# Products of constants in TensorE's waits: norms, feed-forward entries, two recurrence levels and the heads' loop

## The chip, the cores and the metric

The kernel runs on one core of one Trainium2 chip. Its time is the device time of one execution in microseconds (us); of the kernel before, three runs took 2835.75, 2836.42 and 2836.65, median 2836.42. A core has five engines that run their own instruction streams in order and wait for each other by semaphores: TensorE (PE; its weight loads stand as PEld), VectorE (DVE), ScalarE (ACT), GpSimd (POOL) and SyncE (SP), which issues transfers.

## What is computed

Two networks of two layers each, one behind the other, on 256 tokens of width 1024, in f32.

```python
def first_block(x, mem, ...):
    for l in range(2):
        x = x + 0.5 * swiglu(rms_norm(x, ffn1_norm[l]), ffn1_w_gu[l], ffn1_w_down[l])   # 1024 -> 2816 -> 1024
        h = rms_norm(x, mix_norm[l]); z = h @ w_in[l]
        y_a = dilated_attention(...) @ w_att_branch[l]
        o_b = hgrn2_recurrence(...)            # a gated recurrence over the tokens, 8 heads
        x = x + (sigmoid(gate_a) * y_a + sigmoid(gate_b) * y_b) @ w_mix_out[l]
        x = x + cross_attention(rms_norm(x, xattn_norm[l]), rms_norm(mem, mem_norm[l]), ...)
        x = x + 0.5 * swiglu(rms_norm(x, ffn2_norm[l]), ...)
    return rms_norm(x, final_norm)

def second_block(x, c, ...):
    for l in range(2):
        h = rmsnorm(x, norm_g[l, 0]) * (1 + sc1) + sh1
        x = x + 0.5 * g1 * swiglu_2(h, ...)
        h = rmsnorm(x, norm_g[l, 1]) * (1 + sc2) + sh2
        qa, ka, va, qb, kb, vb, qi, ki, wi, qc, kc, vc = split(h @ w_in[l])
        o = concat(moba_attention(qa, ka, va), dsa_attention(qb, kb, vb, qi, ki, wi),
                   stick_breaking_attention(qc, kc, vc))      # 4, 4 and 8 heads of 64
        x = x + g2 * (rms(o) * out_g[l] @ w_out[l])
        h = rmsnorm(x, norm_g[l, 2]) * (1 + sc3) + sh3
        x = x + 0.5 * g3 * swiglu_2(h, ...)
```

## The kernel before

All weights come from HBM as one stream of 1 MB tiles through a ring of four slots. A weight product has f32 accuracy out of three matmuls of a faster format: ScalarE copies a tile to its high part (`w_hi`, L320), VectorE subtracts for the low part (`ring_lo`, L327), and `triple` (L329) multiplies high by high, high by low and low by high. Nearly all of TensorE's work is such triples. Products of two activations, and sums by a constant matrix, are plain f32 matmuls; the trace shows each of these as two matmuls.

Each engine's program is written out by hand in one function per block and engine (`one_pe`, `two_pe`, `two_act` and so on); the order in it is the order on the engine, and `wait_ge` lines set what waits for what.

A norm works on four quarters of `x` (token half b, column half): ScalarE squares them with a running sum (`square`), VectorE forms the variance, both the reciprocal root; VectorE scales a quarter (L598 where there is a shift), TensorE transposes it (`flip_x`, L524: wait for `h_scaled`, four transposes, count `xt_done`), ScalarE copies the transposed quarter to `h_hi` (`h_high`, L391), VectorE subtracts for `h_lo` (L576). The engines do these in an order of their own for each norm. For the norm behind block two's first feed-forward ScalarE's is `shift_z_act` (L509):

```python
            h_high(act, n, 0, 4)
            square(act, n, 2)
            square(act, n, 3)
            rstd_act(act, n, 1)
```

A feed-forward (`ffn_pe`) begins with `first_three` (L832): for the first token half b=0 eight triples over two weight tiles and four over a third, then the transposes of the second half (`flip_x(pe, n, 1, base)`, last where `turn_last` is set, as in block two), then the same triples for b=1. Its four calls in block two are the first and second feed-forward of either layer, called entries below; block one's second feed-forward is the one with `FFN_B`.

`level` (L1268) is one of eight levels of block one's recurrence: TensorE runs two tiles of projections, waits for VectorE's and ScalarE's exponentials (`e_ready`) and multiplies them for eight heads.

The heads' loop of `two_pe` takes eight pairs of heads, one ordinary and one stick-breaking. Per turn TensorE transposes the probabilities of one head into bank 6 (`flip`, L2317), multiplies scores of a later pair, sums the logarithms of the stick-breaking head into bank 1 (`sums`, L2325) and weighs the values. Bank 6 is free again when ScalarE has copied it (L2516, counted by `pt_ready`); the exponentials (L2499) are counted by `exp_ready`. Bank 1 is free when VectorE has taken its argument from it (L2721, `arg_ready`). After every second pair, TensorE transposes the normed outputs back (`turn_back`, L2364).

Of the kernel before, what the change touches and what calls it, by code (L numbers as in the profile page):

```python
# [30 lines left out]
T = 256  # L31
D = 1024
KD = D // P
DEPTH = 2
# [30 lines left out]
FFN_B = X_O + 4  # L65
# [12 lines left out]
FFN_C = 0  # L78
# [7 lines left out]
FFN_D = Z_O + 4  # L86
# [95 lines left out]
def program(nc, x_in, mem_t, pos, c_row, gain_rows, stream, ada, vec, con, lmask, out):  # L182
    with ExitStack() as ctx:
# [105 lines left out]
        S = type("S", (), s)  # L289
# [9 lines left out]
        def nth(which, count):  # L299

            return base.get(which.num, 0) + count
# [27 lines left out]
        def triple(out, w, x, start, stop, group=False):  # L329

            for n, (a, b) in enumerate(((w[0], x[0]), (w[0], x[1]), (w[1], x[0]))):
                mm = nc.tensor.matmul(out, a, b, start=start and n == 0, stop=stop and n == 2,  # L332
                                      skip_group_check=group)
            return mm

        def weights(p, a, b):
# [494 lines left out]

        def first_three(pe, p, n, base, banks, done, turn_last):  # L832

            for b in range(2):
                for k in range(KD):
                    if b == 0 and k % 4 == 0:
                        pe.wait_ge(S.w_lo_ready, p + k // 4 + 1)
                    if k % 4 == 0:
                        pe.wait_ge(S.h_ready, nth(S.h_ready, 4 * n + 2 * b + k // 4 + 1))
# [9 lines left out]
                mm = half_pair(pe, p + 2, 0, (banks[0] + 2, banks[1] + 2), h2, b)  # L849
                if b == 0 and turn_last:  # L850
                    flip_x(pe, n, 1, base)
            mm.then_inc(S.tile_done, 1)
# [32 lines left out]

        def ffn_pe(pe, p0, f, n, shift, between=None, near=None, after=None):

# [25 lines left out]

            first_three(pe, p0, n, 4, (0, 1), S.gu_done, shift)
            if between:
# [335 lines left out]
        def one_pe(pe, l):  # L1251
# [16 lines left out]
            def level(i):  # L1268

                if i < LEVELS:  # L1270
                    pe.wait_ge(S.e_ready, nth(S.e_ready, i + 1))
# [195 lines left out]
            out_pairs(pe, X_O, 4, (o_hi, o_lo), S.att_ready, HEADS, lambda: flip_x(pe, 3, 0, 4))  # L1467
            ffn_pe(pe, FFN_B, 1, 3, False, near=(lambda: flip_x(pe, 4, 0, 4)) if l < DEPTH - 1 else None)

# [718 lines left out]
        pt2 = prob_t  # L2188
        OUT_BANK = (7, 3, 7, 4)
        o_tok = hk[:].rearrange("p k t -> p (k t)").rearrange("p (j n) -> p j n", j=4)  # L2190
        stat = e_buf[1][:].rearrange("p k t -> p (k t)")
# [18 lines left out]
        def two_pe(pe, l):  # L2210
            FFN_C, Z_QI, Z_V, Z_O, FFN_D = tiles_2(l)
            if l == 0:
                flip_x(pe, 0, 0, 4)
            ffn_pe(pe, FFN_C, 0, 0, True, after=lambda: flip_x(pe, 1, 0, 4))

            flip_x(pe, 1, 1, 4)

            def tile(n):
# [98 lines left out]
            def flip(n):  # L2317
                pe.wait_ge(S.exp_ready, nth(S.exp_ready, n + 1))
                if n >= 1:
                    pe.wait_ge(S.pt_ready, nth(S.pt_ready, n))  # L2320
                for c, at in enumerate((0, P, 2 * P)):
                    mm = nc.tensor.transpose(ps[:, 6, c * P:(c + 1) * P], prob_2[n % 3][:, at:at + P], ident)
                mm.then_inc(S.pt_done, 1)

            def sums(c):  # L2325

                pe.wait_ge(S.l_ready, nth(S.l_ready, c + 1))
                if c >= 1:
                    pe.wait_ge(S.arg_ready, nth(S.arg_ready, c))
                ll = st[:, 4 + c % 2, :]  # L2330
                nc.tensor.matmul(ps[:, 1, 0:T], C(C_TRI, P), ll[:, 0:T], start=True, stop=False,
# [95 lines left out]
            flip_x(pe, 2, 0, 4)  # L2427
            ffn_pe(pe, FFN_D, 1, 2, True, after=(lambda: flip_x(pe, 3, 0, 4)) if l < DEPTH - 1 else None)

# [675 lines left out]
```

## Time and profile before

| | |
|---|---|
| profiled execution | 2836.47 us |
| its span, first to last instruction | 2834.4 us |
| PE | 2767.2 us busy, 98% |
| DVE | 1951.5 us, 69% |
| ACT | 1364.6 us, 48% |
| mean granted TensorE clock | 0.991 |

Of the chain of waits that ended last, 83% is TensorE and 9% VectorE. A busy share says that an engine has work at hand, not that it works at full clock: the granted clock stands apart, as a share of 2.4 GHz. In the timeline, a bracket at the end of a row is the time that the engine was idle before it, with what ended the wait. The ends of matmuls are modelled and overlap the next one's start, so of many like matmuls the distance of the starts is the price of one.

### The profile page before, as it was taken

The page shows a single profiled execution, that of the slowest core. Times are in us where ns is not written, and L with a number is a line of the kernel's source. Part 1 is how long each engine was busy: PE and PEld are TensorE (multiplying, and loading weights), DVE is VectorE, ACT ScalarE, POOL GpSimd, SP SyncE. Part 2 cuts the span into 40 slices and gives each one's busy share as a digit, 9 for nine tenths or more (in the row PEclk, how much of TensorE's full clock was granted, in tenths as well). Part 3 has the DMA queues.
Part 4 walks back from the last instruction along what each step waited for, and adds up shares of the span by engine and source line. Part 5 has one row for each costly group of instructions (what it writes and reads, how often), then busy time and mean ns, then how long its engine had stood idle before and what let it go on. Part 6 is the DMA issues. An engine that isn't in the chain of part 4 may idle for free.

```text
span 2834.4 us, 37832 instructions
## 1 busy us (share of the span) xinstructions
PE 2767.2 (98%) x16120; PEld 2426.3 (86%) x16120; DVE 1951.5 (69%) x2187; ACT 1364.6 (48%) x1562; POOL 228.7 (8%) x201
## 2 busy tenths in 40 slices
PE   8999999999999999999999999999999999999999
PEld 6889999998888889999998887888878878788787
DVE  6768876655666678876655667667876676777644
ACT  5444545455445444545455444444644444446433
POOL 0000420000000000420000000003000000030000
PEclk9999999999999999999999999999999999999999
DMA  8655433445776654433446676663266676442554
GB/s 304 258 220 183 153 120 134 171 164 200 267 265 236 257 214 179 149 134 134 162 159 230 254 257 247 253 224 135 103 238 251 246 264 258 183 149 77 197 187 148
DMA packets 82038, 564.42 MB, mean 199 GB/s; under 512 B 9072, under 2 KB 10576, under 8 KB 15952
## 3 DMA queue, kind: packets, MB, share of 16 engines
q1 hardware_dynamic: 66272, 465.47, 44.9%
q0 software_dynamic: 15600, 96.55, 9.1%
q8 instruction: 127, 2.08, 0.3%
q14 instruction: 39, 0.32, 0.0%
HBM read 560.86 MB, written 1.12 MB: 198 GB/s over the span
## 4 chain that ended last, share of the span: by engine, by line
PE 83%; DVE 9%; ACT 3%; POOL 2%; DMA 2%; issue 1%; SPq 0%; POOLq 0%; ACTq 0%; DVEq 0%
PE ps L332 75%; DVE ring_lo L327 3%; ACT w_hi L320 2%; PE ps L899 1%; DMA rows<-mod_rows 1%; POOL qk L2038 1%; PE ps L1287 1%; POOL rope_a L2034 1%; PE ps L530 1%; DVE a_hg L1806 1%; PE ps L1416 0%; PE ps L1442 0%; DVE e L993 0%; DVE e L1786 0%; DVE e L1785 0%
## 5 line engine op out<-in xcount | busy, mean ns | idle before, releaser
L327 DVE TENSOR_TENSOR ring_lo<-ring,w_hi 128x2048 fp32r<-128x2048 f32 x422 | 974.0, 2310 | 478.6 <-ACT w_hi L320 464.2
L320 ACT ACTIVATE w_hi<-ring 128x2048 fp32r<-128x2048 f32 x422 | 806.2, 1910 | 308.5 <-PE ps L332 187.7
L332 PE MATMUL ps<-w_hi,h_hi 128*128 128x512 f32 (+1 forms) x1920 | 731.7, 381 | 17.6 <-DVE h_lo L576 9.2
L332 PE MATMUL ps<-w_hi,h_lo 128*128 128x512 f32 (+1 forms) x1920 | 719.2, 375 | 0.0
L332 PE MATMUL ps<-ring_lo,h_hi 128*128 128x512 f32 (+1 forms) x1920 | 718.7, 374 | 0.0
L332 PEld LDWEIGHTS ps<-w_hi,h_hi 128*128 128x128 f32 x1920 | 365.3, 190 | 84.9 <-DVE ring_lo L327 10.3
L332 PE MATMUL ps<-h_hi,w_hi 128*128 128x256 f32 x1488 | 431.0, 290 | 1.3 <-DVE h_lo L576 1.3
L332 PE MATMUL ps<-h_lo,w_hi 128*128 128x256 f32 x1488 | 422.7, 284 | 0.0
L332 PE MATMUL ps<-h_hi,ring_lo 128*128 128x256 f32 x1488 | 422.6, 284 | 0.0
L332 PEld LDWEIGHTS ps<-w_hi,h_lo 128*128 128x128 f32 x1920 | 364.8, 190 | 65.3
L332 PEld LDWEIGHTS ps<-ring_lo,h_hi 128*128 128x128 f32 x1920 | 365.5, 190 | 61.1 <-issue 1.0
L332 PEld LDWEIGHTS ps<-h_hi,w_hi 128*128 128x128 f32 x1488 | 287.2, 193 | 6.3 <-issue 5.9
L332 PEld LDWEIGHTS ps<-h_lo,w_hi 128*128 128x128 f32 x1488 | 287.4, 193 | 2.8 <-issue 2.4
L332 PEld LDWEIGHTS ps<-h_hi,ring_lo 128*128 128x128 f32 x1488 | 287.1, 193 | 0.0
L332 PE MATMUL ps<-w_hi,g_hi 128*128 128x512 f32 x576 | 224.6, 390 | 1.6 <-DVE g_lo L1083 1.6
L332 PE MATMUL ps<-w_hi,g_lo 128*128 128x512 f32 x576 | 224.1, 389 | 0.0
L332 PE MATMUL ps<-ring_lo,g_hi 128*128 128x512 f32 x576 | 224.1, 389 | 0.0
L993 DVE CUSTOM_DVE_ANT_0 e<-e,val 128x1024 f32<-128x1024 f32 x154 | 181.6, 1220 | 5.7 <-ACT val L1000 5.7
L1041 ACT ACTIVATE g_hi<-ps 128x512 fp32r<-128x512 f32 x80 | 47.7, 597 | 227.6 <-PE ps L899 227.6
L981 POOL DMA_DIRECT2D e<-ada x77 | 40.7, 529 | 1121.8 <-DVE mod_sum L993 826.6
L332 PEld LDWEIGHTS ps<-w_hi,g_hi 128*128 128x128 f32 x576 | 108.1, 188 | 24.7 <-DVE g_lo L1083 2.4
L332 PEld LDWEIGHTS ps<-w_hi,g_lo 128*128 128x128 f32 x576 | 108.1, 188 | 22.5
(359 smaller groups left out, 3430.2 us busy)
## 6 DMA issues: line engine op xcount, KB each, us to landing
ring<-stream SPq DMA_DIRECT2D x438, 1024.0 KB, 4.8
e<-ada POOLq DMA_DIRECT2D x77, 1024.0 KB, 5.9
rows<-mod_rows POOLq DMA_DIRECT2D x18, 512.0 KB, 6.5
rows<-gain_rows POOLq DMA_DIRECT2D x8, 512.0 KB, 4.6
val<-c_row POOLq DMA_DIRECT2D x4, 512.0 KB, 5.2
x<-x_in SPq DMA_DIRECT2D x4, 256.0 KB, 6.7
mem<-mem_t SPq DMA_DIRECT2D x1, 1024.0 KB, 16.1
out_t<-x SPq DMA_DIRECT2D x4, 256.0 KB, 2.1
```

The source lines that it names most:

```text
L320: nc.scalar.activation(hi_of(p), ring[:, p % RING, :], ACT.Copy).then_inc(S.w_hi_ready, 1)
L327: nc.vector.tensor_tensor(lo_of(p), ring[:, p % RING, :], hi_of(p).bitcast(F32), ALU.subtract).then_inc(S.w_lo_ready, 1)
L332: mm = nc.tensor.matmul(out, a, b, start=start and n == 0, stop=stop and n == 2, skip_group_check=group)
L530: mm = nc.tensor.transpose(ps[:, base + q, j * P:(j + 1) * P], xs[:, b, at:at + P], ident)
L899: mm = nc.tensor.transpose(ps[:, bank, a * T + b * P:a * T + (b + 1) * P], g_f[:, i % 2, b, a * P:(a + 1) * P], ident)
L981: pool.dma_start(e_buf[(i + 1) % 2][:].rearrange("p k t -> p (k t)"), ada[l * 2 * PER_FFN + first + i]).then_inc(ada_loaded[(i + done) % 2 ...
L993: ins = nc.vector.tensor_tensor_reduce(part, part, silu_c, 1.0, 0.0, ALU.mult, ALU.add, mod_sum[:, at + n:at + n + 1])
L1041: nc.scalar.activation(g_hi[:, g_slot(i - 1), :], ps[:, 2 * ((i - 1) % 2), :], ACT.Copy).then_inc(S.ghi_ready, 1)
L1287: mm = nc.tensor.matmul(ps[:, 4 + 2 * g + j // 2, at:at + n], sta[:, hd, t * P:(t + 1) * P], right, start=True, stop=True)
L1806: ins = nc.vector.copy_predicated(dst.rearrange("p a (g two c) -> p a g two c", two=2, c=c)[:, :, :, 1, :], upper(mask, c).unsqueeze(1).br ...
L2034: nc.gpsimd.tensor_tensor(rope_a[:], part, cos1[:].unsqueeze(1).broadcast_to([P, 2, T]), ALU.mult).then_inc(S.pool_chain, 1)
L2038: nc.gpsimd.tensor_tensor(part, rope_a[:], turned[n % 2][:], ALU.add).then_inc(S.rope_done, 1)
```

## The change

`hold_clock(bank, count)` issues `count` products on TensorE: the constant identity matrix as the stationary side, 256 columns of the constants' table as the moving side, into a bank whose content nobody reads before it is written anew. They depend on no data and count no semaphore. 95 of them are put in:

- at recurrence levels 2 and 3, two each, ahead of the wait for `e_ready`, in both layers of block one (8);
- in block one's second feed-forward, two ahead of the first wait for `h_ready`, in both layers (4);
- in block two, layer 0: seven ahead of the first transposes; in `first_three` of the four entries 3, 0 or 1, and 2: ahead of the first half, ahead of the second half's transposes (1 but for the first entry), ahead of the second half;
- behind the first feed-forward (`z_flip`): eight ahead of the first half's transposes, two ahead of and two behind the second half's, in both layers; three ahead of the next layer's norm (once);
- in the heads' loop, ahead of the transposes of heads 1, 5, 6 and 7 (3, 3, 2, 3) and ahead of the sums of head 6 (2), in both layers. There the two waits of `flip` and of `sums` change places: first the one that frees the bank, then the products, then the other.

```diff
+        def hold_clock(bank, count):
+            for _ in range(count):
+                nc.tensor.matmul(ps[:, bank, 0:T], ident, con_sb[:, 0:T], start=True, stop=True,
+                                 skip_group_check=True)
...
-        def first_three(pe, p, n, base, banks, done, turn_last):
+        def first_three(pe, p, n, base, banks, done, turn_last, hold):
             for b in range(2):
                 for k in range(KD):
                     if b == 0 and k % 4 == 0:
                         pe.wait_ge(S.w_lo_ready, p + k // 4 + 1)
+                    if k == 0:
+                        hold_clock(banks[b], hold[2 * b])
                     if k % 4 == 0:
                         pe.wait_ge(S.h_ready, nth(S.h_ready, 4 * n + 2 * b + k // 4 + 1))
...
                 if b == 0 and turn_last:
+                    hold_clock(banks[1], hold[1])
                     flip_x(pe, n, 1, base)
...
             def level(i):
+                if i in (2, 3):
+                    hold_clock(3, 2)
                 if i < LEVELS:
                     pe.wait_ge(S.e_ready, nth(S.e_ready, i + 1))
...
-            ffn_pe(pe, FFN_B, 1, 3, False, near=(lambda: flip_x(pe, 4, 0, 4)) if l < DEPTH - 1 else None)
+            ffn_pe(pe, FFN_B, 1, 3, False, near=(lambda: flip_x(pe, 4, 0, 4)) if l < DEPTH - 1 else None, hold=(2, 0, 0))
...
+        HOLD_FLIP, HOLD_SUMS = {1: 3, 5: 3, 6: 2, 7: 3}, {6: 2}
...
             if l == 0:
+                hold_clock(3, 7)
                 flip_x(pe, 0, 0, 4)
-            ffn_pe(pe, FFN_C, 0, 0, True, after=lambda: flip_x(pe, 1, 0, 4))
+            def z_flip():
+                hold_clock(3, 8)
+                flip_x(pe, 1, 0, 4)
+            ffn_pe(pe, FFN_C, 0, 0, True, after=z_flip, hold=(3, 0 if l == 0 else 1, 2))
+            hold_clock(3, 2)
             flip_x(pe, 1, 1, 4)
+            hold_clock(3, 2)
...
             def flip(n):
-                pe.wait_ge(S.exp_ready, nth(S.exp_ready, n + 1))
                 if n >= 1:
                     pe.wait_ge(S.pt_ready, nth(S.pt_ready, n))
+                hold_clock(6, HOLD_FLIP.get(n, 0))
+                pe.wait_ge(S.exp_ready, nth(S.exp_ready, n + 1))
...
             def sums(c):
-                pe.wait_ge(S.l_ready, nth(S.l_ready, c + 1))
                 if c >= 1:
                     pe.wait_ge(S.arg_ready, nth(S.arg_ready, c))
+                hold_clock(1, HOLD_SUMS.get(c, 0))
+                pe.wait_ge(S.l_ready, nth(S.l_ready, c + 1))
...
-            ffn_pe(pe, FFN_D, 1, 2, True, after=(lambda: flip_x(pe, 3, 0, 4)) if l < DEPTH - 1 else None)
+            def next_flip():
+                hold_clock(3, 3)
+                flip_x(pe, 3, 0, 4)
+            ffn_pe(pe, FFN_D, 1, 2, True, after=next_flip if l < DEPTH - 1 else None, hold=(3, 1, 2))
```

Two places of TensorE's order. The first is the end of block two's first feed-forward. Before, the last down product (`w_hi`, `g_lo`) is followed by the transposes of the four quarters, each behind its own `h_scaled`, and by the projections:

```order
L332 MATMUL ps<-w_hi,g_lo 128x512
L530 MATMUL ps<-con_sb,e 128x128 [waits h_scaled]
L530 MATMUL ps<-con_sb,e 128x128 x3
L530 MATMUL ps<-con_sb,e 128x128 [waits h_scaled]
L530 MATMUL ps<-con_sb,e 128x128 x3
L530 MATMUL ps<-con_sb,e 128x128 [waits h_scaled]
```

With the change (the products are L339, the transposes have become L536):

```order
L332 MATMUL ps<-w_hi,g_lo 128x512
L339 MATMUL ps<-con_sb 128x256 x8
L536 MATMUL ps<-con_sb,e 128x128 [waits h_scaled]
L536 MATMUL ps<-con_sb,e 128x128 x3
L536 MATMUL ps<-con_sb,e 128x128 [waits h_scaled]
L536 MATMUL ps<-con_sb,e 128x128 x3
L339 MATMUL ps<-con_sb 128x256 x2
L536 MATMUL ps<-con_sb,e 128x128 [waits h_scaled]
```

The eight stand ahead of the first quarter, two between the second and the third. The other place is the heads' loop. Before, at the transposes of head 6 and its sums:

```order
L2355 MATMUL ps<-val,a_hg 128x64
L2322 MATMUL ps<-con_sb,prob_66 128x128 [waits pt_ready,exp_ready]
L2322 MATMUL ps<-con_sb,prob_66 128x128 x2
L2331 MATMUL ps<-a_hg,con_sb 128x256 [waits arg_ready,l_ready]
L2333 MATMUL ps<-a_hg,con_sb 128x128
```

With the change:

```order
L2377 MATMUL ps<-val,a_hg 128x64
L339 MATMUL ps<-con_sb 128x256 [waits pt_ready]
L339 MATMUL ps<-con_sb 128x256
L2343 MATMUL ps<-con_sb,prob_66 128x128 [waits exp_ready]
L2343 MATMUL ps<-con_sb,prob_66 128x128 x2
L339 MATMUL ps<-con_sb 128x256 [waits arg_ready]
L339 MATMUL ps<-con_sb 128x256
L2353 MATMUL ps<-a_hg,con_sb 128x256 [waits l_ready]
```

The products have taken over the wait for the bank; the transposes and the sums keep the wait for their data.

## Rows read from the trace of the kernel before

**Rows 1.** Windows at half clock: stretch, length, busy time per engine (count), granted clock, transfers.

```profile
368.46:375.28 6.82, 6.82 (x34) 6.82 (x33) 6.38 (x3) 5.31 (x8) 6.46 (x4) 0.50 0.19 78
...
sum 51.19, PE 43.43 PEld 37.91 DVE 41.72 ACT 27.03 POOL 6.46; mean PE 6.20 PEld 5.42 DVE 5.96 ACT 3.86 POOL 0.92
```

**Rows 2.** TensorE's groups by shape: count, busy us, mean ns, idle before.

```profile
L1156 PE MATMUL ps<-hb,con_sb 128*128 128x256 f32 x16 | 3.6, 379 | 0.0
```

**Rows 3.** Timeline, TensorE, recurrence level 2: start, us, instruction, idle before it.

```profile
366.71 0.55 PE L1287 MATMUL ps<-e 128*128 128x64 f32 x3 [1.10 <-DVE e L1786]
```

**Rows 4.** Windows, level 2 to the second feed-forward, both layers.

```profile
366.71:685.87 319.16, 318.11 (x2336) 303.80 (x2336) 202.48 (x202) 158.20 (x185) 16.48 (x10) 0.99 0.42 153
1214.19:1532.20 318.01, 315.46 (x2336) 300.75 (x2336) 202.41 (x202) 158.17 (x185) 16.48 (x10) 1.00 0.43 156
```

**Rows 5.** Timeline, TensorE, block one's second feed-forward, second weight tile.

```profile
685.87 0.50 PE L332 MATMUL ps<-w_hi,h_hi 128*128 128x512 f32 x1 [0.99 <-DVE ring_lo L327]
```

**Rows 6.** Timeline, TensorE, block two's first norm and entry.

```profile
1718.66 1.32 PE L530 MATMUL ps<-con_sb,e 128*128 128x128 f32 x8 [3.09 <-DVE e L2137]
1721.34 0.77 PE L332 MATMUL ps<-w_hi,h_hi 128*128 128x512 f32 x1 [1.36 <-DVE h_lo L576]
```

**Rows 7.** Windows, first half of three entries of block two.

```profile
1721.34:1734.27 12.93, 11.95 (x44) 9.49 (x44) 11.52 (x23) 5.07 (x12) 0.53 (x1) 0.78 0.00 0
2084.41:2095.39 10.98, 9.76 (x44) 7.45 (x45) 10.02 (x15) 4.19 (x10) 0.53 (x1) 1.00 0.09 38
2276.16:2288.05 11.89, 10.91 (x45) 8.75 (x45) 10.02 (x15) 4.18 (x10) 0.53 (x1) 0.86 0.03 13
```

**Rows 8.** Timeline, VectorE, scaling of the second half in block two's first entry.

```profile
1729.94 1.42 DVE L2137 SCALAR_TENSOR_TENSOR e<-e,small,rows 128x512 f32<-128x512 f32 x2
```

**Rows 9.** Timeline, TensorE, second half's transposes in the entry that began at 2084.41.

```profile
2093.38 1.16 PE L530 MATMUL ps<-con_sb,e 128*128 128x128 f32 x8
```

**Rows 10.** Timeline, TensorE, the norm behind block two's first feed-forward, layer 0.

```profile
1911.09 0.60 PE L530 MATMUL ps<-con_sb,e 128*128 128x128 f32 x4
1915.48 1.11 PE L530 MATMUL ps<-con_sb,e 128*128 128x128 f32 x4 [3.79 <-DVE e L598]
1917.32 1.97 PE L530 MATMUL ps<-con_sb,e 128*128 128x128 f32 x8 [0.73 <-DVE e L598]
```

**Rows 11.** Timeline, ScalarE, the same norm.

```profile
1911.73 0.60 ACT L395 ACTIVATE h_hi<-ps 128x512 fp32r<-128x512 f32 x1 [0.90 <-PE ps L530]
1912.74 0.63 ACT L381 ACTIVATE e<-x 128x512 f32<-128x512 f32 x1 [0.42 <-DVE x L731]
```

**Rows 12.** Timeline, VectorE, the same norm's second variance.

```profile
1914.55 0.21 DVE L556 TENSOR_SCALAR nrm<-nrm 128x1 f32<-128x1 f32 x1
```

**Rows 13.** Windows, the projections behind it: two stretches of one length.

```profile
1919.94:1924.93 4.99, 4.99 (x23) 4.99 (x24) 4.97 (x3) 1.28 (x1) 0.00 (x0) 0.50 0.02 3
1924.93:1929.92 4.99, 4.99 (x44) 4.99 (x43) 0.56 (x4) 1.76 (x2) 1.01 (x1) 1.00 0.11 18
```

**Rows 14.** Timeline, TensorE, heads' loop, layer 0: heads 1, 6, sums 6, head 7.

```profile
2028.08 0.52 PE L2322 MATMUL ps<-con_sb,prob 128*128 128x128 f32 x3 [1.67 <-ACT prob_t L2516]
...
2048.36 0.52 PE L2322 MATMUL ps<-con_sb,prob 128*128 128x128 f32 x3 [1.07 <-ACT prob_t L2516]
2049.87 0.67 PE L2331 MATMUL ps<-a_hg,con_sb 128*128 128x256 f32 x2 [1.00 <-DVE a_hg L2721]
...
2054.12 0.52 PE L2322 MATMUL ps<-con_sb,prob 128*128 128x128 f32 x3 [1.40 <-ACT prob_t L2516]
```

**Rows 15.** Timeline, ScalarE, heads' loop: exponentials of head 1, copy of head 0.

```profile
2023.06 0.50 ACT L2499 ACTIVATE prob<-prob,small 128x256 f32<-128x256 f32 x1
...
2027.45 0.48 ACT L2516 ACTIVATE prob_t<-ps 128x384 f32<-128x384 f32 x1
```

**Rows 16.** Windows, head 1 to the next norm, both layers.

```profile
2028.08:2081.73 53.65, 48.20 (x303) 40.38 (x303) 37.13 (x84) 34.31 (x86) 2.09 (x4) 1.00 0.26 91
2581.47:2638.91 57.44, 52.31 (x304) 43.74 (x304) 37.15 (x84) 34.44 (x86) 1.57 (x3) 0.91 0.22 74
```

More of the change, by code:

```diff
@@ L884, in out_ready, with ffn_pe @@
             return wait
-        def ffn_pe(pe, p0, f, n, shift, between=None, near=None, after=None):
+        def ffn_pe(pe, p0, f, n, shift, between=None, near=None, after=None, hold=(0, 0, 0)):
             def gate_up(i, half, p, b):
@@ L912, in down @@
                 return mm
-            first_three(pe, p0, n, 4, (0, 1), S.gu_done, shift)
+            first_three(pe, p0, n, 4, (0, 1), S.gu_done, shift, hold)
             if between:
```

## The prediction

> **What bounds the kernel now.** I read the page's busy times first, then the windows over the stretches at the lower clock, then the timeline of each place that gets products, one engine at a time, and last the same stage in two layers beside each other. The reader is to see three things. TensorE is busy 98% of the span (the table of the page), so what can be won is small: its waits, and the time that it works at the lower clock. That clock is granted in seven stretches of 51.19 us in all, at 0.50, the lower of its two levels, that is 1.2 instead of 2.4 GHz [rows 1]. And a wait is worth filling only at its own place in TensorE's order: in front of the instruction that waits, behind nothing else that another engine needs.
>
> **The price of one product.** The nearest row is eight products of 256 columns, f32 with a constant stationary side, which the trace shows as 16 matmuls [rows 2]. 3.6 us less the 0.38 that the last one takes, over 15 steps, is 0.215 us a matmul, so 0.43 a product at full clock and at most twice that, 0.86, at half. The change adds 95 products, 41 us; the question at each place is whether they lie in idle time.
>
> **Recurrence levels (8 products).** Two products, 0.86 us, stand ahead of the level's wait on VectorE, which is 1.10 us [rows 3]. They fit: cost nothing. In layer 0 the clock fell just behind this wait, in layer 1 it did not, though the wait is the same. From this level to the second feed-forward the layers took 319.16 and 318.01 us at mean clocks of 0.99 and 1.00 [rows 4]. So of a stretch of 6.8 us at half clock only 1.15 us reaches the end; the level products are paced by VectorE, which catches up meanwhile. Gain 1.15.
>
> **The two products in the first block's second feed-forward (4 in all).** They delay the first twelve products of the half by 0.86 us, and those are followed by a wait of 0.99 us for the second weight tile, which VectorE makes on its own time [rows 5]. The wait takes the 0.86 back: nothing. If not, 4 x 0.43 = 1.7 us.
>
> **Block two's entries.** In layer 0 seven products (3.01 us) go into a wait of 3.09, and three (1.29) into one of 1.36 [rows 6]: free. The first half of the entry took 12.93 us at a clock of 0.78, where the same half at 1.00 took 10.98, and 11.89 at 0.86 in two others (the fourth, 11.88, reads like the third) [rows 7]. Layer 0 cannot win the whole 1.95: VectorE's second pair of scaled quarters ends at 1729.94 + 1.42 = 1731.36 [rows 8], and the transposes of the last quarter (four, 0.60 us in rows 10) would end at about 1731.95 instead of 1733.3. Gain 1.3. The other two win 0.9 each. Three products ahead of the next layer's norm lie in a wait of 1.1 us and the tenth or two that a matmul's drawn end overlaps its successor: nothing. The pair ahead of the second half of each entry stands in front of a wait for VectorE's remainder of about its own length: nothing.
> Against that stands the single product ahead of the transposes of the second half, at three entries. The transposes start there without a wait [rows 9], so each product moves them, ScalarE's copy and VectorE's remainder behind them: 3 x 0.43 = 1.3 lost.
>
> **The norm behind the first feed-forward of block two (12 products a layer).** This is one place where the fill misses its wait. TensorE's wait of 3.79 us lies between the first quarter's transposes (1911.09) and the second quarter's (1915.48), not ahead of the first [rows 10]. The eight products stand ahead of the first. They take 3.44 us, so these transposes run from 1914.53 to 1915.13. ScalarE copies that quarter (in before at 1911.73) before it may square the third and fourth quarters (from 1912.74) [rows 11], and VectorE's variance (1914.55) waits for both squares [rows 12]. The copy starts at 1915.17, the squares end at about 1917.04, the variance comes at 1917.1, 2.5 us late, and the second quarter's scaling follows it. So TensorE gets its second quarter at 1918.0 and has waited 2.9 us: the wait is moved behind the fill, not filled.
> What the clock does then decides. In before the project products after this norm ran 23 in 4.99 us at half clock and 44 in the next 4.99 at full [rows 13]; the missing 21 are 2.4 us. If the clock stays up, the entry is 2.5 later, the last eight transposes 0.7 faster (1.97 against 1.16 to 1.32 elsewhere [rows 6, 9]), the products 2.4 faster: 2.4 + 0.7 - 2.5, some 0.5, is won. If it falls again behind a wait of 2.9 (it fell behind 3.09 and 3.79), the second quarter's transposes take 1.11 instead of 0.60, each pair of products 1.72 instead of 0.86, and up to 2.5 is lost. I take 1.2 lost a layer, nearer to the fall: 2.4 in all.
>
> **The heads' loop (13 products a layer).** The other place. TensorE's waits here are 1.67, 1.40, 1.07, 1.40 us ahead of the transposes of the probabilities and 1.00 ahead of the sums (the 1.40 of the fifth head reads like the seventh's) [rows 14]. In before each of these transposes waited for two things: the exponentials and ScalarE's copy of the head before. The exponentials were long done (2023.06 for the wait that ended at 2028.08); the copy came last (2027.45 + 0.48) [rows 15]. In the change the products stand behind the wait for that copy, since they write its bank. So the wait stays as long as it was, and the products come on top of it. The same holds for the sums: the wait that ended last was VectorE's argument, and the two products stand behind it.
> Summed along TensorE: head 1, 1.29. Head 5, 1.29, of which head 6's wait of 1.07, set by ScalarE, takes back 1.07: 0.22. Head 6, 0.86 more, makes 1.08, of which the sums' wait of 1.00 takes back 1.00: 0.08. The sums, 0.86. Head 7, 1.29; behind it TensorE runs the output projection without a wait. Together 3.5 a layer; between head 1 and head 5 some starts are a tenth late and may take back 0.3, so I take 3.2 a layer, 6.4 in all, with 2.9 to 5.6 (each product in full) as bounds.
> What is won: from head 1 to the next norm layer 0 took 53.65 us at 1.00 and layer 1 57.44 at 0.91 [rows 16]. With more work in the stretches ahead of the fall I expect layer 1 to run like layer 0: 3.8 won.
>
> **The sum.** Won: 1.15 + 1.3 + 0.9 + 0.9 + 3.8 = 8.05. Lost: 1.3 + 2.4 + 6.4 = 10.1. Net 2.05 slower, on the profiled execution's 2836.47 (span 2834.4 and 2.1 around it; 0.05 over the median): 2838.5 us. On its own this has a range of 2834 to 2843.5: the loop's upper bound on the one side, both norms at their better end on the other.
>
> **One rule weighed.** The pairs of layers price the half clock: 1.15 us for a stretch of 6.8, 3.8 for one of 10.24, 0.9 for one of 3.41, so between a sixth and two fifths of the time [rows 1, 4, 7, 16]. The Trainium skill, TensorE: Matmul & The Clock Gate, Terms, gives the penalty as the throttled time times the lost share of pulses, a half; by that all stretches together cost 25.6 us. The trace agrees only where nothing but TensorE sets the pace.
>
> **Rivals.**
> 1. The fills are free also in the loop and at the norm: ScalarE, busy nearly without a break there, sets the pace, and TensorE's delay vanishes in it. For it: the waits do end on ScalarE. Against: what ScalarE copies last is itself TensorE's transposes. Then 2836.47 - 8.05 + 1.3 - 1.0 = 2828.7. Chance 0.16.
> 2. The whole half-clock time comes back: 51.19 / 2 = 25.6 won [rows 1], and the loop and the single products lost, 7.7: 2818.6. (This is the result of the rule just named.) Against: the pairs above. Chance 0.03.
> 3. Slower: in the loop the wait of 1.40 ahead of head 7 is left as it was, and the clock falls behind it all the same, in layer 1 or in both. Price 3.8 a layer that is not won (2842.3), or lost in layer 0 as well (2846.1). It decides as soon as either layer's stretch has a mean clock under 1.00. For it: the wait keeps its length; against: there are 1.29 us of dense work behind it and 0.86 ahead. Chance 0.22.
> 4. The change doesn't do what it says: constants against an identity do not keep the clock, nothing is won, and 1.3 + 6.4 + 5.0 are lost: 2849.2. Against: the loop's f32 products of constants are followed by a full clock in layer 0. Chance 0.05.
>
> **How the numbers follow.** The forecast has 0.54. About 0.2%, 5.7 us, is what a measurement of this kernel can tell from no change. Faster (under 2830.8): 0.13 of rival 1, rival 2 and a rest of the forecast, 0.17. Slower (over 2842.1): most of rival 3, rival 4 and a rest, 0.25. Within: 0.58. The range 2829 to 2846 reaches to rival 1 and takes in rival 3.
>
> **What would show it.** Right: the eight products stand ahead of a wait of some 3 us between the first and second quarter's transposes at both norms; the waits of 1.40 before heads 5 and 7 are still there, ended by ScalarE's copy, with three products behind them; head 1 to the next norm takes some 57 us in both layers at a clock of 1.00; the first half of block two's entries takes 11.0 to 11.6. Wrong: a loop stretch near 54 us (rival 1), one over 60 (rival 3), or low stretches that stand where they stood (rival 4). What breaks the forecast most easily is the clock behind the moved wait at the two norms.

## The result and the profile after

The changed kernel took 2839.53 us (median of 22 executions, 2836.55 to 2844.62). The kernel before took 2834.54 on the same chip (22 executions, 2829.04 to 2840.01). The ratio is 1.0019, 95% interval 1.0014 to 1.0025. By the medians the change costs 5.0 us; the forecast was 2838.5 us, a cost of 2.05. (The ratios here and below come with their intervals; they are not the quotients of the two medians, from which they differ by up to 0.0008.)

| | before | after |
|---|---|---|
| profiled execution | 2836.47 us | 2841.83 us |
| its span | 2834.4 us | 2839.8 us |
| PE busy | 2767.2 us, 98% | 2789.8 us, 98% |
| mean granted clock | 0.991 | 0.999 |

**The clock.** Of the seven low stretches of before, 51.19 us [rows 1], one of 3.41 us is left up to TensorE's last product. The windows view shows it at half clock:

```profile
1919.53:1922.95 3.42, 3.42 (x14) 2.93 (x13) 2.61 (x4) 2.12 (x3) 0.00 (x0) 0.50 0.00 0
```

Over all executions the median granted clock is 0.998 with the change (22 executions) and 0.992 in before (27 executions, timed beside e1 to e4). So the products do keep the clock up, and the time rises all the same: they cost more than the clock gives back.

**The norm behind block two's first feed-forward, layer 0**, TensorE's timeline (start, us, instruction, idle before it; L339 are the products, L536 the transposes; the matrix products L332 left out). It answers to [rows 10]:

```profile
1912.15 3.61 PE L339 MATMUL ps<-con_sb 128*128 128x256 f32 x16
1915.60 0.60 PE L536 MATMUL ps<-con_sb,e 128*128 128x128 f32 x4
1919.09 0.74 PE L536 MATMUL ps<-con_sb,e 128*128 128x128 f32 x4 [2.88 <-DVE e L604]
...
1921.33 1.83 PE L536 MATMUL ps<-con_sb,e 128*128 128x128 f32 x8
```

Eight products, 3.45 us from start to start, push the first quarter's transposes back, and a wait of 2.88 stands behind them: moved, not filled. The windows from the last product ahead of the norm to one and the same product of the projections, both layers of before, then of after:

```profile
1910.86:1930.00 19.14, 13.97 (x83) 12.87 (x82) 13.29 (x21) 8.94 (x14) 1.09 (x1) 0.73 0.28 103
2464.63:2483.41 18.78, 13.62 (x84) 12.51 (x82) 13.29 (x21) 8.94 (x14) 1.16 (x1) 0.73 0.28 103
```

```profile
1911.92:1931.76 19.84, 16.95 (x108) 15.42 (x107) 13.29 (x21) 8.83 (x14) 1.10 (x1) 0.91 0.27 99
2470.15:2489.18 19.03, 15.81 (x107) 13.98 (x106) 13.26 (x21) 8.82 (x14) 1.16 (x1) 1.00 0.27 102
```

The clock (third number from the right) went from 0.73 to 0.91 and 1.00, and the stretch is longer, by 0.70 and 0.25 us.

**The heads' loop, layer 0**, TensorE's timeline: the products of heads 1 (with its transposes), 5 and 6, those ahead of head 6's sums, and those of head 7. It answers to [rows 14]:

```profile
2029.75 1.56 PE L339 MATMUL ps<-con_sb 128*128 128x256 f32 x6 [1.59 <-ACT prob_t L2543]
2031.15 0.49 PE L2343 MATMUL ps<-con_sb,prob 128*128 128x128 f32 x3
...
2047.21 1.56 PE L339 MATMUL ps<-con_sb 128*128 128x256 f32 x6 [1.31 <-ACT prob_t L2543]
...
2051.11 1.08 PE L339 MATMUL ps<-con_sb 128*128 128x256 f32 x4
...
2052.49 1.13 PE L339 MATMUL ps<-con_sb 128*128 128x256 f32 x4
...
2057.53 1.56 PE L339 MATMUL ps<-con_sb 128*128 128x256 f32 x6 [1.31 <-ACT prob_t L2543]
```

The waits of 1.67, 1.40 and 1.40 are there as 1.59, 1.31 and 1.31, ended by ScalarE's copy as before, and the products stand behind them. The windows of the loop, from the score products ahead of head 1's transposes to the last product ahead of the next norm, both layers, before and then after:

```profile
2024.41:2080.83 56.42, 49.81 (x317) 41.84 (x317) 39.90 (x89) 37.05 (x91) 2.09 (x4) 1.00 0.28 98
2577.80:2638.34 60.54, 53.92 (x317) 45.19 (x317) 40.21 (x90) 37.51 (x91) 1.57 (x3) 0.92 0.24 83
```

```profile
2026.17:2085.62 59.45, 55.24 (x344) 46.59 (x343) 39.46 (x85) 36.34 (x88) 2.09 (x4) 1.00 0.26 93
2583.59:2643.01 59.42, 55.23 (x343) 46.58 (x343) 39.65 (x86) 36.40 (x89) 1.57 (x3) 1.00 0.24 85
```

Layer 0 is 3.03 longer at the same clock; layer 1 is 1.12 shorter, since its low stretch is gone.

**What the forecast did not have.** Behind the loop TensorE waits for the next norm's first quarter. VectorE's work for it begins only when the rows of the modulation are there, which GpSimd's queue reads (L2839; L2812 in before). TensorE's wait was 0.51 us in layer 0 of before. In after:

```profile
2087.76 1.32 PE L536 MATMUL ps<-con_sb,e 128*128 128x128 f32 x8 [1.75 <-DVE e L604]
```

The reads landed later: from the transfer view around the last two of layer 0's loop, before and then after (KB each, median us from issue to landing).

```profile
rows<-mod_rows POOLq DMA_DIRECT2D x2, 512.0 KB, 7.5
```

```profile
rows<-mod_rows POOLq DMA_DIRECT2D x2, 512.0 KB, 8.1
```

The last one alone took 9.54 us instead of 8.31. With TensorE's instructions of both traces matched one by one, the two waits behind the loops and a third ahead of block two cost 1.2, 1.2 and 1.8 us, 4.2 of the 5.4 between the two profiled executions. Two more waits stand in this profile and not in that of before, the second behind a tile of the stream that ScalarE got late; they put TensorE 0.9 and 1.1 us further behind:

```profile
1315.01 1.20 PE L1362 MATMUL ps<-con_sb,prob 128*128 128x128 f32 x9 [0.88 <-DVE prob L1914]
...
1749.42 0.50 PE L332 MATMUL ps<-w_hi,g_hi 128*128 128x512 f32 x1 [0.84 <-DVE g_lo L1092]
```

These five waits take more than the whole 5.4. Whether they belong to the kernel is asked in the last experiment.

### The profile page after: what moved, and what is told of

It reads as the page before. It is cut to its first block, busy times and chain, and to the rows that moved or that the text cites. A ratio compares the mean times of both kernels' runs of the same rounds, so it can differ in the third digit from the quotient of the medians.

```text
span 2839.8 us, 38196 instructions
## 1 busy us (share of the span) xinstructions
PE 2789.8 (98%) x16310; PEld 2444.4 (86%) x16310; DVE 1951.6 (69%) x2187; ACT 1365.0 (48%) x1562; POOL 228.9 (8%) x201
## 3 DMA queue, kind: packets, MB, share of 16 engines
HBM read 560.86 MB, written 1.12 MB: 198 GB/s over the span
## 4 chain that ended last, share of the span: by engine, by line
PE 81%; DVE 10%; ACT 4%; POOL 2%; DMA 2%; issue 1%; SPq 0%; POOLq 0%; ACTq 0%; DVEq 0%
PE ps L332 72%; DVE ring_lo L327 4%; ACT w_hi L320 2%; POOL qk L2049 1%; PE ps L908 1%; DMA rows<-mod_rows 1%; PE ps L339 1%; POOL rope_a L2045 1%; PE ps L536 1%; DVE a_hg L1817 1%; DVE e L1797 1%; DVE e L1796 1%; PE ps L1298 1%; DMA ring<-stream 1%; PE ps L1427 0%
## 5 line engine op out<-in xcount | busy, mean ns | idle before, releaser
L332 PE MATMUL ps<-w_hi,h_hi 128*128 128x512 f32 (+1 forms) x1920 | 728.4, 379 | 8.7 <-DVE ring_lo L327 7.4
L332 PE MATMUL ps<-w_hi,h_lo 128*128 128x512 f32 (+1 forms) x1920 | 715.7, 373 | 0.0
L332 PE MATMUL ps<-ring_lo,h_hi 128*128 128x512 f32 (+1 forms) x1920 | 714.5, 372 | 0.0
L332 PEld LDWEIGHTS ps<-w_hi,h_hi 128*128 128x128 f32 x1920 | 362.3, 189 | 78.2 <-DVE ring_lo L327 12.0
L332 PE MATMUL ps<-h_hi,w_hi 128*128 128x256 f32 x1488 | 429.0, 288 | 0.0
L332 PE MATMUL ps<-h_hi,ring_lo 128*128 128x256 f32 x1488 | 420.9, 283 | 0.0
L332 PE MATMUL ps<-h_lo,w_hi 128*128 128x256 f32 x1488 | 420.9, 283 | 0.0
L332 PEld LDWEIGHTS ps<-w_hi,h_lo 128*128 128x128 f32 x1920 | 362.1, 189 | 64.6
L332 PEld LDWEIGHTS ps<-ring_lo,h_hi 128*128 128x128 f32 x1920 | 362.6, 189 | 60.4 <-issue 1.0
L332 PEld LDWEIGHTS ps<-h_hi,w_hi 128*128 128x128 f32 x1488 | 285.3, 192 | 4.8 <-issue 4.4
L332 PEld LDWEIGHTS ps<-h_lo,w_hi 128*128 128x128 f32 x1488 | 285.3, 192 | 2.8 <-issue 2.4
L332 PEld LDWEIGHTS ps<-h_hi,ring_lo 128*128 128x128 f32 x1488 | 285.3, 192 | 0.0
L332 PE MATMUL ps<-w_hi,g_hi 128*128 128x512 f32 x576 | 224.7, 390 | 2.4 <-DVE g_lo L1092 2.4
L332 PE MATMUL ps<-w_hi,g_lo 128*128 128x512 f32 x576 | 224.1, 389 | 0.0
L332 PE MATMUL ps<-ring_lo,g_hi 128*128 128x512 f32 x576 | 224.1, 389 | 0.0
L332 PEld LDWEIGHTS ps<-w_hi,g_hi 128*128 128x128 f32 x576 | 108.1, 188 | 26.0 <-DVE g_lo L1092 3.7
L332 PEld LDWEIGHTS ps<-w_hi,g_lo 128*128 128x128 f32 x576 | 108.1, 188 | 22.4
```

## Experiments

Unless a line says otherwise, every edit is to the changed kernel. "Loop" is the last pair of windows above, "norm" the pair before. The kernel before was timed beside these runs: 2833.69 us beside e1 to e4, 2833.92 beside e5 to e8, 2835.61 beside e9 to e11.

### Norm: the eight products behind the first quarter (e3)

```diff
-def flip_x(pe, n, b, base):
+def flip_x(pe, n, b, base, fill=0):
     for q in (2 * b, 2 * b + 1):
+        if q % 2 == 1:
+            hold_clock(3, fill)
...
-    hold_clock(3, 8)
-    flip_x(pe, 1, 0, 4)
+    flip_x(pe, 1, 0, 4, 8)
```

> The changed kernel with the eight products of the norm behind block two's first feed-forward moved from ahead of the first quarter's transposes to between the first and the second quarter's, where the wait is. Theory A: the place decides. The first quarter goes out 3.44 us earlier, ScalarE's copy, VectorE's variance and the second quarter's scaling with it, and the wait behind it is filled (0.3 to 0.5 us of it left): at each of the two norms the entry comes some 2.5 us earlier at an unchanged clock. The profile of the changed kernel shows the two norms at +0.82 and +0.26 us against before, so they become -1.7 and -2.2, and the time is 4 to 5 us below the changed kernel, 2834.5 to 2835.5. Theory B: the eight products pay by the clock alone and a wait of 2.9 us behind them does no harm: no change, within 1 us. Theory C: VectorE's chain, which starts with the statistics and not with the first quarter, sets the second quarter's time, and the gain is under 1.5 us in all.

2833.52 us, ratio to before 0.9991 (0.9983 to 1.0000), where the changed kernel has 1.0019. Its timeline and its windows of both norms:

```profile
1912.68 0.60 PE L538 MATMUL ps<-con_sb,e 128*128 128x128 f32 x4
1913.12 3.62 PE L339 MATMUL ps<-con_sb 128*128 128x256 f32 x16
1917.07 0.66 PE L538 MATMUL ps<-con_sb,e 128*128 128x128 f32 x4 [0.33 <-DVE e L606]
```

```profile
1912.45:1928.93 16.48, 15.82 (x107) 13.87 (x106) 13.25 (x21) 8.94 (x14) 1.09 (x1) 1.00 0.32 119
2465.59:2482.08 16.49, 15.82 (x107) 13.88 (x106) 13.26 (x21) 8.94 (x14) 1.16 (x1) 1.00 0.32 121
```

The same sixteen matmuls now lie in the wait; 0.33 of it is left. Against the norm of after at the same clock, 19.03, that is 2.54 us a layer: theory A. The time lies 1.0 us below A's range. B, no change, and C, a gain under 1.5 us, fall.

### Norm: without the eight (e5)

```diff
 def z_flip():
-    hold_clock(3, 8)
     flip_x(pe, 1, 0, 4)
```

> The changed kernel without the eight products at the norm behind block two's first feed-forward (the two pairs behind it stay). Theory A: ahead of the first quarter the eight cost the entry about as much as the clock gives back: without them the first quarter goes out 3.44 us earlier, TensorE waits 3.8 again between the quarters, the clock falls behind that wait at both norms (two or three low stretches, 6.8 to 10.2 us, each), and the time is within 2.4 us of the changed kernel on the lower side (the forecast's 1.2 a layer): 2837 to 2839.5. Theory B: the eight are worth the whole clock there, 2 to 3 us a layer: 2843 to 2845. Theory C: they are pure delay: 2833.

2834.79 us, ratio 1.0006 (0.9997 to 1.0014). The wait is 3.79 again, but the clock fell for one stretch of 3.41 us at each norm, not for two or three:

```profile
1911.87:1929.36 17.49, 13.38 (x92) 12.32 (x90) 13.28 (x21) 8.94 (x14) 1.09 (x1) 0.90 0.31 113
2466.13:2483.72 17.59, 13.63 (x92) 12.40 (x90) 13.20 (x21) 8.83 (x14) 1.16 (x1) 0.90 0.30 117
```

So none at all is better than eight in the wrong place by 2.35 and 1.44 us, and eight in the right place better than none by 1.0 and 1.1. My range missed; the time lies between A and C, nearer to C. The low stretch was 10.24 us at both norms of before; here the pairs around the second half stay, and it is 3.41. That the pairs shorten it is likely, but no run takes them away alone.

### Loop: no products (e1)

```diff
-HOLD_FLIP, HOLD_SUMS = {1: 3, 5: 3, 6: 2, 7: 3}, {6: 2}
+HOLD_FLIP, HOLD_SUMS = {}, {}
```

> The changed kernel without the 13 products of the heads' loop (the order of the waits stays as changed). Theory A: the products behind the wait for ScalarE's copy are added to that wait, so without them each layer's loop is shorter by about 3.1 us (the profile of the changed kernel has 3.06 in layer 0): the stretch from head 1 to the next norm is 53.5 to 54 us where the clock stays at 1.00, and the time is about 6 us below the changed kernel, 2833.5; if the clock falls in one layer's loop as it did in the kernel before, 3.8 of it are lost again, 2837. Theory B: ScalarE sets the pace of the loop and TensorE's delay vanishes in it: same time as the changed kernel, within 1 us.

2837.93 us, ratio 1.0009 (1.0000 to 1.0019). Its loops:

```profile
2024.68:2085.09 60.41, 54.05 (x317) 45.34 (x317) 40.12 (x90) 37.40 (x91) 2.10 (x4) 0.92 0.26 92
2582.60:2638.85 56.25, 51.33 (x317) 43.27 (x317) 40.51 (x90) 37.59 (x91) 1.58 (x3) 0.97 0.26 89
```

The delay is real: layer 1 is 3.17 us shorter without the products, although its clock fell for 3.41 us. In layer 0 the clock fell for 10.24 us, which costs 4.2, more than the 3.03 that the products cost. The median is near the 2837 that A named for one fall, but the time alone does not tell A from B: the intervals of this kernel and of the changed one, 1.0000 to 1.0019 and 1.0014 to 1.0025, overlap. The loops tell them apart.

### Loop: its products alone, on the kernel before (e2)

The kernel before with `HOLD_FLIP`, `HOLD_SUMS` and the new order of the waits in `flip` and `sums`.

> The kernel before with the 13 products of the loop alone. Theory A: 3.1 us a layer longer, 6.2 in all, less 3.8 for each layer whose loop would have run at the lower clock: between 2837 and 2841, so 2.4 to 6.2 us slower than before, and the waits of 1.40 ahead of heads 5 and 7 stay at 1.3 to 1.4 with the products behind them. Theory B: no change against before, within 1 us.

2834.66 us, ratio 1.0002 (0.9994 to 1.0011). Loops 59.46 and 59.47, no low stretch in either: the 3.03 of theory A in both layers. The time is the one that theory B named, within 1 us of before, and lies below A's range. So A is shown for the loop by the trace, and its account of the whole time missed: what the products add, the clock gives back. The median granted clock is 0.995 here and 0.992 in the executions of before timed beside it.

### Three misplacements mended, six products in the loop (e4)

To the edits of the moved eight come: no single product at block two's entries, level products at level 5 alone, and in the loop:

```diff
-HOLD_FLIP, HOLD_SUMS = {1: 3, 5: 3, 6: 2, 7: 3}, {6: 2}
+HOLD_FLIP, HOLD_SUMS = {1: (3, 3), 5: (1, 1), 7: (1, 2)}, {}
...
+    if n in HOLD_FLIP:
+        if n == 1:
+            pe.wait_ge(S.evac_done, nth(S.evac_done, 14))
+        else:
+            pe.wait_ge(S.arg_ready, nth(S.arg_ready, n))
+        hold_clock(*HOLD_FLIP[n])
     if n >= 1:
         pe.wait_ge(S.pt_ready, nth(S.pt_ready, n))
-    hold_clock(6, HOLD_FLIP.get(n, 0))
```

> Only fills that lie inside a wait of their own. Level products ahead of level 5 (where the kernel before waits 1.10 us) instead of levels 2 and 3; no single product ahead of the second half's transposes at block two's entries; the eight products moved behind the first quarter; in the loop three products in an empty bank ahead of the wait for ScalarE's copy at head 1, one at head 5 and two at head 7, none at head 6 and ahead of the sums. The rest as changed. Theory A: against the changed kernel -1.3 for the singles, -4 to -5 for the norms, -6 for the loop, levels 0: 2827 to 2829.5, which is 5 to 7.5 us below the kernel before, if the clock falls nowhere. If one loop falls, 3.8 more. Theory B (ScalarE and the transfers pace these places): 2837 to 2840, no change against the changed kernel.

2825.13 us (5 executions), ratio 0.9966 (0.9953 to 0.9978), 2 us below the range of A. The loops take 57.89 us with a low stretch of 3.41, and 56.25 without.

### The same with the loop's products behind the waits (e7), and with none (e8)

To the kernel of e4:

```diff
-HOLD_FLIP, HOLD_SUMS = {1: (3, 3), 5: (1, 1), 7: (1, 2)}, {}
+HOLD_FLIP, HOLD_SUMS = {1: 3, 5: 3, 6: 2, 7: 3}, {6: 2}
```

and `{}, {}` for the second, both with the products' lines where the change has them.

> The kernel of e4 (2825.1) with the loop's products as the change has them: 13 a layer, behind the waits for ScalarE's copy and VectorE's argument, in place of six a layer ahead of those waits. Theory A: the place decides here too: the clock is held by either, and the products behind the waits add 3.1 us a layer: 2831, and the waits of 1.3 are back ahead of the products of heads 5 and 7. Theory B: the loop's delay is absorbed by ScalarE or by the rows' transfer behind the loop: 2825 to 2827.

> The kernel of e4 without any product in the loop. Theory A: the loop's waits are back at 1.67, 1.40, 1.07, 1.00, 1.40 and the clock falls once or twice in each layer's loop or just behind it, as it did without the loop's products in the changed kernel (10.24 us in one layer, 3.41 in the other): 1 to 4 us a layer, so 2827 to 2833. Theory B: the loop is paced by ScalarE at either clock: 2825. With e7 it prices the loop's products: behind the waits they pay only if this kernel is slower than e7.

Behind: 2830.85 us, ratio 0.9989 (0.9980 to 0.9997), loops 59.47 twice at full clock. None: 2830.50 us, ratio 0.9990 (0.9981 to 0.9999), and loops

```profile
2020.19:2080.24 60.05, 53.69 (x317) 45.09 (x317) 40.52 (x90) 37.68 (x91) 2.09 (x4) 0.91 0.26 93
2573.03:2633.20 60.17, 53.82 (x318) 45.14 (x317) 40.20 (x90) 37.47 (x91) 1.57 (x3) 0.91 0.24 83
```

Theory A both times. By e7 and e8 thirteen products behind the waits are worth nothing: they cost 3.0 a layer, and save what the clock would have cost, which is 3.8 and 3.9 here, and was nothing in layer 0 of before and 4.3 in layer 1.

### Two small edits alone (e6)

```diff
-    if i in (2, 3):
+    if i == 5:
...
-ffn_pe(pe, FFN_C, 0, 0, True, after=z_flip, hold=(3, 0 if l == 0 else 1, 2))
+ffn_pe(pe, FFN_C, 0, 0, True, after=z_flip, hold=(3, 0, 2))
...
-ffn_pe(pe, FFN_D, 1, 2, True, after=next_flip if l < DEPTH - 1 else None, hold=(3, 1, 2))
+ffn_pe(pe, FFN_D, 1, 2, True, after=next_flip if l < DEPTH - 1 else None, hold=(3, 0, 2))
```

> The changed kernel with two edits: the level products ahead of level 5 alone instead of levels 2 and 3, and no single product ahead of the transposes of the second half at block two's entries. Theory A: the level products that stood at levels 2 and 3 without a wait were taken back by the waits of levels 4 and 5, so moving them changes nothing; at level 5 the two products fill the wait of 1.10 and the clock stays up behind it as well. The three singles are gone: -1.3. Together 2838 (1.3 below the changed kernel). Theory B: TensorE's delay at levels 2 and 3 runs through to the end: -3.4 more for two layers, 2835. Theory C: products at level 5 alone do not hold the clock: +1.2 a layer, 2840.5.

2836.93 us, ratio 1.0014 (1.0005 to 1.0023). The interval does not tell A from B or C. The trace does for the singles: each entry that loses its product is 0.42 to 0.44 us shorter (first halves of 11.07 to 11.09 instead of 11.50 and 11.51). For the levels it does not support A: in layer 0 the clock fell behind the levels with the products at level 5, too.

### All thirteen ahead of the waits (e9, e10)

```diff
+    if n in HOLD_FLIP:
+        if n == 1:
+            pe.wait_ge(S.evac_done, nth(S.evac_done, 14))
+        else:
+            pe.wait_ge(S.scores_read, nth(S.scores_read, HEADS_2 - 1))
+        hold_clock(3 if n == 1 else 4, HOLD_FLIP[n])
     if n >= 1:
         pe.wait_ge(S.pt_ready, nth(S.pt_ready, n))
-    hold_clock(6, HOLD_FLIP.get(n, 0))
...
 def sums(c):
+    hold_clock(4, HOLD_SUMS.get(c, 0))
     if c >= 1:
         pe.wait_ge(S.arg_ready, nth(S.arg_ready, c))
-    hold_clock(1, HOLD_SUMS.get(c, 0))
```

On the kernel of e4 (its other edits kept):

> The kernel of e4 with the loop's 13 products a layer at the change's five places (heads 1, 5, 6, the sums of head 6, head 7), all ahead of the wait there, in a bank that is empty by then (the bank of head 6's scores, read 1.3 us earlier). Theory A: the same products that cost 3.03 us a layer behind the waits cost nothing ahead of them and hold the clock in both layers: the stretch from head 1's transposes to the last product before the norm is 56.3 to 56.6 us in both layers (e4: 57.88 with one low stretch, and 56.26), and the time is 2823.5 to 2825.5. Theory B: products that fill a wait to within 0.1 or 0.2 us make the copy's successor late, some 0.2 us at each of five places: 58 us a layer, 2827 to 2828.

On the changed kernel, this edit alone:

> The changed kernel with that one edit alone: the loop's 13 products ahead of the waits in an empty bank. Theory A: 3.0 us a layer less than the changed kernel at the same clock, 6 in all: 2833.5 if the changed kernel takes 2839.5. Theory B: as the changed kernel, within 1 us.

The first took 2825.18 us (5 executions), ratio 0.9957 (0.9945 to 0.9970). The second took 2831.97, ratio 0.9991 (0.9982 to 1.0000), 7.5 us below the changed kernel beside it (e11), where A had 6; its loops are 56.25 and 56.26. The first one's products and transposes of heads 1 and 5, and its loops:

```profile
2024.08 1.46 PE L339 MATMUL ps<-con_sb 128*128 128x256 f32 x6
2025.82 0.55 PE L2349 MATMUL ps<-con_sb,prob 128*128 128x128 f32 x3 [0.29 <-ACT prob_t L2549]
...
2040.83 1.46 PE L339 MATMUL ps<-con_sb 128*128 128x256 f32 x6
2042.31 0.55 PE L2349 MATMUL ps<-con_sb,prob 128*128 128x128 f32 x3
```

```profile
2022.24:2078.49 56.25, 55.57 (x344) 46.14 (x343) 39.50 (x86) 36.37 (x90) 2.09 (x4) 1.00 0.28 99
2572.52:2628.75 56.23, 55.57 (x344) 46.13 (x343) 40.54 (x90) 37.59 (x91) 1.57 (x3) 1.00 0.25 89
```

The same 13 products cost nothing and hold the clock: theory A. e4 and e9 are the fastest and beat both kernels; against the kernel before timed beside them they take 8.6 and 10.4 us less.

### The changed kernel once more (e11)

No edit.

> The changed kernel once more, to see which of its profile's extra times belong to the kernel. In the profiled execution the reads of the rows of the modulation ended 1.2 us later behind each loop and 1.8 later ahead of block two than in nine other kernels' profiles. Theory A: that belonged to the one execution: here the last product before the norm is followed by a wait of 0.4 to 0.9 us as in the others, the span is 3 to 4 us shorter than the changed kernel's 2839.8, and the median is 2837 to 2839.5. Theory B: the changed kernel's own timing makes them late: 1.8 to 2.1 us again behind both loops, median 2839.5 or more.

2839.50 us, the same median as the first time. The ratio is 1.0008 (0.9999 to 1.0017): by the medians the change costs 3.9 us here instead of 5.0, and this interval does not exclude that it costs nothing. The profiled execution took 2836.72, span 2834.6. The wait behind layer 0's loop is now

```profile
2083.19 0.99 PE L536 MATMUL ps<-con_sb,e 128*128 128x128 f32 x5 [0.72 <-DVE e L604]
```

and from the last product to that start it is 1.11 us in layer 0 and 0.36 in layer 1 (2.14 and 1.79 in the first profile). The wait ahead of block two is 0.35 instead of 1.87, and those of 0.88 and 0.84 are not there (a wait like the second stands in the profile of e3, 0.87). So theory A for the waits: they were that execution's. The median does not decide, since it lies where the two theories meet. The executions of this kernel lie between 2836.4 and 2844.6; the first profile caught one above the median, this one a fast one.

## Why the prediction came out as it did

The place of the fill decides, as forecast, at the norm and in the loop, and there the sizes held too. That the forecast lies only 1.0 us from the median is in part luck, since other terms were off and what the executions scatter by was not in it. Point by point:

- **One product, 0.43 us.** The eight took 3.45: right.
- **Recurrence: a misreading.** The wait of 1.10 [rows 3] stands ahead of level 5, not level 2, and [rows 4] begins there too. At levels 2 and 3, where the products went, there is no wait. TensorE's timeline at level 3 of after (L1298 is the level):

```profile
334.84 1.03 PE L339 MATMUL ps<-con_sb 128*128 128x256 f32 x4
335.70 0.55 PE L1298 MATMUL ps<-e 128*128 128x64 f32 x4
```

  Each pair costs 0.87, and the waits ahead of levels 4 and 5 take 0.49 and 1.25 of it back: the cost of nothing was right for another reason. The 1.15 that the clock should give came in after [rows 4]: 317.99 instead of 319.16. It did not come in others with the same level products. The same stretch in the kernel without products in the loop, and in the repeat:

```profile
365.94:686.39 320.45, 319.22 (x2342) 304.55 (x2341) 202.52 (x202) 158.11 (x185) 16.47 (x10) 0.99 0.43 153
```

```profile
365.75:683.73 317.98, 316.35 (x2342) 301.48 (x2340) 202.39 (x202) 158.11 (x185) 16.49 (x10) 1.00 0.43 154
```

  In the first of these the clock fell for 6.83 us from about 385, later than in before, and the stretch is 1.3 longer than there. In layer 0 it fell in four of the six profiles with the products at levels 2 and 3, in one of the five with them at level 5, and in e2, which has none. In layer 1 it fell in e2, in e9 and in e10. What decides there stays open.
- **Block one's second feed-forward.** 0.9 lost, and the wait of [rows 5], of which 0.08 is left, takes all of it back in both layers: right.
- **Entries.** The later ones' first halves took 11.51 and 11.50 and were expected at 11.4, with the single product at 0.43: right. The first took 12.34, not 11.6:

```profile
1721.86:1734.20 12.34, 11.02 (x50) 8.01 (x49) 11.52 (x23) 5.88 (x12) 0.69 (x1) 1.00 0.00 0
```

  The gain was 0.6 of the 1.3. The forecast had TensorE's transposes behind VectorE's scaling as the limit. But VectorE's order has four more instructions (1.67 us) between this scaling and the remainder that the second half waits for. Its timeline in before, then in after:

```profile
1731.27 1.67 DVE L2142 TENSOR_SCALAR x<-mem,nrm 128x512 f32<-128x512 f32 x4
1733.53 1.29 DVE L576 TENSOR_TENSOR h_lo<-ps,h_hi 128x512 fp32r<-128x512 f32 x2 [0.59 <-ACT h_hi L395]
```

```profile
1731.88 1.67 DVE L2153 TENSOR_SCALAR x<-mem,nrm 128x512 f32<-128x512 f32 x4
1733.46 1.28 DVE L582 TENSOR_TENSOR h_lo<-ps,h_hi 128x512 fp32r<-128x512 f32 x2
```

  VectorE waited 0.59 us ahead of the remainder in before and not at all in after. By this order that 0.59 was all there was to win.
- **Norm.** The moved wait (2.88 for 2.9) and the delay at one clock (2.54 for 2.5) are as worked out. Net I took 1.2 lost a layer; it was 0.70 and 0.25, and in the repeat 0.80 and 1.08 (19.94 and 19.86 us). Where the clock stayed up (layer 1 of after, layer 0 of e1, e6 and e10) the stretch is 19.03 or 19.04, against 19.14 and 18.78: the gain of 0.5 that the forecast had for that case was 0.1 in layer 0 and a loss of 0.25 in layer 1.
- **Loop.** 3.03 a layer at one clock for 3.2; in layer 1 the fall cost 60.54 - 56.25 = 4.3 (forecast 3.8; 56.25 is layer 1 of e4, at full clock). By the measure of [rows 16], from head 1's transposes to the next norm, the loops of after take 56.6 and 56.2 us, those of the repeat 55.6 and 54.8, where the forecast had some 57.
- **The start.** The forecast counted from a profiled execution with a mean clock of 0.991. Over the 27 executions of before beside e1 to e4 the time goes with the clock: nine at 0.991 average 2836.5, two at 0.995 average 2829.0, and the median of all is 2833.7. (That is 1.9 us for 0.001, which is 5.7 us at half clock: a third, within the sixth to two fifths of the prediction.) So less clock is to be won in the typical execution than in the profiled one: the three medians of before beside the experiments lie 0.9 to 2.8 us under it. The changed kernel scatters too: the median of the repeat's eleven executions, at a clock of 0.998, lies 2.8 over its profiled one at 0.999. Both together are the likeliest reason for a loss of 4 to 5 us; this was read from the spread, not tested by itself. From profile to profile the repeat loses 1.2 us on TensorE between 300 us, ahead of the first product, and the end, where the sum had 2.05.
- **The sum's own range.** By its terms, the loop's upper bound and both norms at their better end, it is 2835.1 to 2843.3, where the forecast has 2834 to 2843.5.

The rivals: 1 falls, fills in the loop and at the norm are free only in another place (and ScalarE, which it calls busy nearly without a break, is busy 37.05 of the 56.42 us of layer 0's loop); 2 falls, with the delays that were found taken out 8.6 to 10.4 us come back, not 25.6; 3 did not happen in after, and of the 14 loops in seven profiles with the products behind the waits one has a low stretch; 4 falls, the clock is 0.999. (The 25.6 was the result of the rule in the Trainium skill, TensorE: Matmul & The Clock Gate, Terms: the penalty is the throttled time times the lost share of pulses. The measured 8.6 to 10.4 us disagree with it.)

From the changed kernel to the one with all thirteen ahead it is 14.3 us by the medians: 6.1 for two loops, 5.1 for two norms, 1.3 for three singles, and 1.8 that is not told apart.

## What to carry to other kernels

A product that is to fill a wait has to be issued ahead of everything that waits there, so it needs a bank that is already empty: behind the wait it is simply added (3.03 us a layer against 0 for the same thirteen). Ahead of a producer it delays the chain that the next wait hangs on, and moves that wait. What the clock costs in one profiled execution is one draw; look at its spread over executions before counting it as a gain.

## What was not expected of the hardware

- The price of a low stretch depends on where it falls. In the loop 3.41 us at 0.50 cost 0 (e1, layer 1: 56.25), 1.64 (e4, layer 0: 57.89) or 1.66 (e5, layer 1: 61.12 against 59.46); 10.24 us cost 3.8 to 4.3.
- The reads of the rows scatter. The last one behind a loop took 6.6 to 9.5 us over 13 profiles, although it was always issued 2.85 us behind one tile of the stream and 4.34 to 4.37 ahead of the next. Up to 1.8 us of that reached TensorE.
